# Six norms: feature sums gathered beside the last linear layer's tiles, roots computed with tokens on partitions

## The reference, cut to what matters

```python
def layer_norm(x, g, b):
    mu = jnp.mean(xf, -1, keepdims=True)
    var = jnp.mean(jnp.square(xf - mu), -1, keepdims=True)
    return (xf - mu) * lax.rsqrt(var + NORM_EPS) * g + b
def rms_norm(x, g):
    return xf * lax.rsqrt(jnp.mean(xf * xf, -1, keepdims=True) + EPS) * g
# first_block, i = 0 (attention), 1 (s5):
x = layer_norm(alpha * x + gate * ((y * silu(z)) @ w_out[i]), ln_g[i], ln_b[i])
# hybrid_layer, layer = 0, 1:
hl = rms_norm(xl, norm_mix) * (1.0 + sc1_l) + sh1_l
...
xl = xl + g1_l * (jnp.concatenate([att_l, ml_l, pool_l], -1) @ w_out)
h2l = rms_norm(xl, norm_ffn) * (1.0 + sc2_l) + sh2_l
xl = xl + g2_l * ((silu(h2l @ w_g) * (h2l @ w_u)) @ w_d)
# at the end
return rms_norm(xl, final_norm)
```

## Time and profile before

| | |
|---|---|
| median of three runs | 2534.68 us |
| the three runs | 2533.98, 2534.68, 2544.10 us |
| the profiled execution | 2543.55 us, of it 2541.7 us span |
| granted TensorE clock, mean | 0.921 of full |

### The profile page before, as it was taken

How to read it: one execution, slowest core, us unless ns; L and a number is a source line. 1 busy time by engine, 2 the same in 40 slices (tenths; PEclk the granted TensorE clock), 3 DMA queues, 4 the chain that set the end, 5 groups by cost and what they waited for, 6 DMA issues and landing times.

```text
span 2541.7 us, 33862 instructions
## 1 busy us (share of the span) xinstructions
PE 2211.3 (87%) x13593; PEld 1672.4 (66%) x13593; DVE 1337.6 (53%) x2599; ACT 906.5 (36%) x1779; POOL 443.0 (17%) x417
## 2 busy tenths in 40 slices
PE   6979798879989995699898976889999997878998
PEld 5757576647546694599463433678888764547997
DVE  4648686565479847364425356443333244455554
ACT  3234454552222363353222444232222212444443
POOL 0047878509821000000000000000000000000000
PEclk8979898989999997899899987989999998978999
DMA  8154444685687646865621212322323422224653
GB/s 285 65 183 129 143 144 111 189 258 166 204 267 229 203 150 246 285 183 164 198 68 50 86 48 84 126 89 84 99 84 94 121 83 83 83 83 135 197 161 105
DMA packets 434035, 366.34 MB, mean 144 GB/s; under 512 B 66238, under 2 KB 412622, under 8 KB 431702
## 3 DMA queue, kind: packets, MB, share of 16 engines
q1 hardware_dynamic: 392212, 320.87, 40.9%
q0 software_dynamic: 7424, 26.38, 2.8%
q10 hardware_dynamic: 34242, 16.92, 2.3%
HBM read 317.58 MB, written 54.92 MB: 147 GB/s over the span
## 4 chain that ended last, share of the span: by engine, by line
PE 69%; DVE 14%; DMA 6%; ACT 6%; POOL 3%; issue 2%; ACTq 1%; SPq 0%; DVEq 0%; POOLq 0%
PE ps L119 66%; DVE A L88 3%; PE ps L122 3%; ACT A L115 3%; POOL A L88 3%; DVE R L88 2%; DVE A L102 2%; DMA wbuf<-ctab 2%; DVE A L92 1%; DVE A L105 1%; DVE A L93 1%; DMA wbuf<-in_ada_w 1%; DMA A<-btab 1%; DVE A L96 1%; ACT A L116 1%
## 5 line engine op out<-in xcount | busy, mean ns | idle before, releaser
L119 PE MATMUL ps<-R,R 128*128 128x256 f32 (+1 forms) x3968 | 849.0, 336 | 33.5 <-ACT R L115 23.4
L119 PEld LDWEIGHTS ps<-R,R 128*128 128x128 f32 x3968 | 634.7, 194 | 108.1 <-ACT R L115 28.6
L119 PE MATMUL ps<-HR,R 128*128 128x512 f32 (+1 forms) x1984 | 557.8, 365 | 35.4 <-DVE R L88 24.8
L88 DVE TENSOR_TENSOR R<-wbuf,R 128x1024 fp32r<-128x1024 f32 (+2 forms) x304 | 349.5, 1158 | 368.0 <-ACT R L115 367.8
L119 PEld LDWEIGHTS ps<-HR,R 128*128 128x128 f32 x1984 | 358.9, 194 | 94.7 <-issue 28.5
L115 ACT ACTIVATE A<-ps 128x512 f32<-128x512 f32 (+4 forms) x400 | 210.3, 556 | 583.9 <-PE ps L119 419.3
L115 ACT ACTIVATE R<-wbuf 128x1024 fp32r<-128x1024 f32 (+2 forms) x304 | 270.1, 894 | 293.6 <-PE ps L119 266.9
L88 DVE TENSOR_TENSOR A<-A 128x128 f32<-128x128 f32 (+4 forms) x868 | 320.6, 400 | 88.1 <-ACT A L115 58.6
L119 PE MATMUL ps<-H,wbuf 128*128 128x512 f32 (+2 forms) x928 | 336.6, 520 | 13.8 <-DVE H L93 13.8
L119 PE MATMUL ps<-A 128*128 128x64 f32 (+10 forms) x1736 | 290.0, 369 | 33.3 <-DVE A L88 7.6
L88 POOL TENSOR_TENSOR A<-A 128x512 f32<-128x512 f32 (+3 forms) x186 | 215.4, 1170 | 528.2 <-DVE A L96 268.4
(11 more groups left out here) (103 smaller groups left out, 1644.0 us busy)
## 6 DMA issues: line engine op xcount, KB each, us to landing
wbuf<-in_w_ada SPq DMA_DIRECT2D x48, 1024.0 KB, 5.2
wbuf<-in_ada_w SPq DMA_DIRECT2D x24, 1024.0 KB, 8.5
wbuf<-in_w_out SPq DMA_DIRECT2D x24, 1024.0 KB, 5.7
wbuf<-in_w_ffn_gate SPq DMA_DIRECT2D x22, 1024.0 KB, 5.3
wbuf<-in_w_ffn_up SPq DMA_DIRECT2D x22, 1024.0 KB, 5.7
wbuf<-in_w_ffn_down SPq DMA_DIRECT2D x32, 704.0 KB, 4.7
wbuf<-in_attn_w_in SPq DMA_DIRECT2D x20, 1024.0 KB, 7.0
ctab<-A ACTq DMA_DIRECT2D x64, 256.0 KB, 2.8
```

The costliest lines, as they stand in the source:

```text
L88: return self.op(lambda e: e.tensor_tensor(out, a, b, op))
L119: return self.op(lambda e: e.matmul(out, lhsT, rhs, start=start, stop=stop, skip_group_check=True))
```

## The change

Six of the seven norms change; `b0m1`, whose context half comes from a load, stays.

- **Gather.** The tiles of `out1`, `out2`, `b0out`, `b1out`, `fd0` and `fd1` get `after` work. In the RMS norms ACT squares tile m into `H` and DVE adds tiles 0 to 5 into one accumulator `ACC`, five additions; tiles 6 and 7 stay apart. In the LayerNorms DVE adds `X` tiles 0 to 5 themselves.
- **LayerNorm.** The mean takes three products (`ACC`, `X` 6, `X` 7) in place of eight. The rest is as before.
- **RMS sums.** The squares are now the stationary side and two columns of ones the moving side, so the sums stand with tokens on partitions: 12 products of 2 columns for 512 tokens, 6 for 256, the last third waiting for tile 7's square.
- **Roots.** Scaling, root and reciprocal work on 128x4 or 128x2 in `SM`. DVE multiplies the identity by them into a diagonal `DG` (128 x width), and one product with `ones` spreads it to all partitions, into a PSUM bank that the loop over the eight tiles reads in place of SBUF.
- **Order.** The root moves ahead of `backlog`; one step of `backlog` stands between the sums and the spreading product, and one fewer behind it.

The diff, cut to its core:

```diff
+        SQG, ACC, DG, RT = H[:, 0:2, :], H[:, 2, :], H[:, 3, :], SM[:, 48:52]
+        class Gather:
+            def __init__(self, name, tiles, m, c0, squares):
+                self.name, self.tiles, self.m, self.c0, self.squares = name, tiles, m, c0, squares
+            def act(self, act):
+                m, c0 = self.m, self.c0
+                if self.squares:
+                    act.wait_ge(dve_evac, (self.tiles, m))
+                    if m > 2:
+                        act.wait_ge(dve_step, (self.name, "acc", min(m - 2, 5)))
+                    act.act((ACC if m == 0 else SQG[:, m % 2, :])[:, c0:512], X[:, m, c0:512], ACT.Square
+                            ).then_inc(act_step, (self.name, "sq", m))
+            def dve(self, dve):
+                m, c0 = self.m, self.c0
+                if 1 <= m <= 5:
+                    first, x = ACC, X[:, m, :]
+                    if self.squares:
+                        dve.wait_ge(act_step, (self.name, "sq", m))
+                        x = SQG[:, m % 2, :]
+                    elif m == 1:
+                        first = X[:, 0, :]
+                    dve.wait_ge(dve_evac, (self.tiles, m))
+                    if m > 1:
+                        dve.wait_ge(dve_step, (self.name, "acc", m - 1))
+                    dve.tt(ACC[:, c0:512], first[:, c0:512], x[:, c0:512], ADD).then_inc(dve_step, (self.name, "acc", m))
+            def pe(self, pe):
+                pass
...
+        def gathered_pe(pe, name, c0):
+            p = PS.take(pe, (name, "ss"), (dve_evac, (name, "rs")))
+            for i, (src, ready) in enumerate([(ACC, (dve_step, (name, "acc", 5))), (SQG[:, 0, :], (act_step, (name, "sq", 6))),
+                                              (SQG[:, 1, :], (act_step, (name, "sq", 7)))]):
+                pe.wait_ge(*ready)
+                for j in range(c0 // 128, 4):
+                    x = pe.mm(p[:, 2 * j:2 * j + 2], src[:, 128 * j:128 * j + 128], ones[:, 0:2], i == 0 and j == c0 // 128, i == 2)
+            x.then_inc(mm_done, (name, "ss"))
+        def gathered_dve(dve, name, c0, eps):
+            n = 4 - c0 // 128
+            rt = RT[:, 0:n]
+            dve.wait_ge(mm_done, (name, "ss"))
+            src = PS[name, "ss"][:, 2 * (4 - n):8].rearrange("p (j x) -> p j x", x=2)[:, :, 0]
+            dve.ts(rt, src, 1.0 / D, eps, MUL, ADD).then_inc(dve_evac, (name, "rs"))
+            dve.wait_ge(act_step, (name, "rs"))
+            dve.recip(rt, rt).then_inc(dve_step)
+            dve.wait_own()
+            dve.tt(DG[:, 0:128 * n].rearrange("p (j c) -> p j c", j=n), ident.unsqueeze(1).to_broadcast([128, n, 128]),
+                   rt.unsqueeze(2).to_broadcast([128, n, 128]), MUL).then_inc(dve_step, (name, "dg"))
+        def spread_pe(pe, name, c0, last):
+            p = PS.take(pe, (name, "rb"), last)
+            pe.wait_ge(dve_step, (name, "dg"))
+            pe.mm(p[:, c0:512], ones, DG[:, 0:512 - c0], True, True).then_inc(mm_done, (name, "rb"))
         class LayerNorm:
...
+                self.name, self.c0, self.g, self.bcol, self.SQ, self.RS, self.tiles = name, c0, g, bcol, SQ, RS, tiles
             def pe(self, pe):
                 p = PS.take(pe, (self.name, "mu"), (dve_step, (self.name, "d", 7)))
-                for k in range(8):
-                    pe.wait_ge(*self.ready(k))
-                    x = pe.mm(p[:, self.c0:512], ones, X[:, k, self.c0:512], k == 0, k == 7)
+                pe.wait_ge(dve_step, (self.name, "acc", 5))
+                pe.mm(p[:, self.c0:512], ones, ACC[:, self.c0:512], True, False)
+                for k in (6, 7):
+                    pe.wait_ge(dve_evac, (self.tiles, k))
+                    x = pe.mm(p[:, self.c0:512], ones, X[:, k, self.c0:512], False, k == 7)
                 x.then_inc(mm_done, (self.name, "mu"))
                 yield
...
-        def out_tile(name, w, K, m, hi, lo, n, c0, M, gate, ready, tx):
+        def out_tile(name, w, K, m, hi, lo, n, c0, M, gate, ready, tx, norm, squares=True):
             return Tile((name, m), w, K, 128 * m, n, lambda k: hi[:, k, :], lambda k: lo[:, k, :], ready, dve_evac,
-                        dve=lambda dve, p: dve_residual(dve, name, m, p, c0, M, gate, tx))
+                        dve=lambda dve, p: dve_residual(dve, name, m, p, c0, M, gate, tx),
+                        after=Gather(norm, name, m, c0, squares))
...
-                sumsq_pe(pe, "fin", 256, self.SQ)
+                gathered_pe(pe, "fin", 256)
+                spread_pe(pe, "fin", 256, (dve_step, ("fin", 7)))
...
-                act.wait_mark("end")
-                sumsq_act(act, "fin", 256, self.SQ, lambda k: (dve_evac, ("fd1", k)))
-                rsqrt_act(act, self.RS[:, 256:512], ("fin", "rs"))
+                rsqrt_act(act, RT[:, 0:2], ("fin", "rs"))
...
             def dve(self, dve):
                 dve.wait_mark("end")
-                dve.wait_ge(mm_done, ("fin", "ss", 7))
-                rsqrt_dve(dve, self.RS[:, 256:512], PS["fin", "ss"][:, 256:512], D, 1e-6, ("fin", "rs"))
-                dve.wait_ge(dve_step, ("fin", "rs"))
+                gathered_dve(dve, "fin", 256, 1e-6)
+                dve.wait_ge(mm_done, ("fin", "rb"))
                 for k in range(8):
-                    dve.stt(X[:, k, 256:512], X[:, k, 256:512], vec(2, 16 + k), self.RS[:, 256:512], MUL, MUL
+                    dve.stt(X[:, k, 256:512], X[:, k, 256:512], vec(2, 16 + k), PS["fin", "rb"][:, 256:512], MUL, MUL
                             ).then_inc(dve_step, ("fin", k))
...
             def pe(self, pe):
-                sumsq_pe(pe, self.name, self.cc, SQ)
+                if self.ready:
+                    sumsq_pe(pe, self.name, self.cc, SQ)
+                else:
+                    gathered_pe(pe, self.name, self.cc)
+            def pe2(self, pe):
+                if not self.ready:
+                    spread_pe(pe, self.name, self.cc, (dve_step, (self.name, 7)))
...
             def act(self, act):
+                if not self.ready:
+                    rsqrt_act(act, RT[:, 0:4 - self.cc // 128], (self.name, "rs"))
+                    return
...
             def act2(self, act):
-                rsqrt_act(act, RS[:, self.cc:512], (self.name, "rs"))
+                if self.ready:
+                    rsqrt_act(act, RS[:, self.cc:512], (self.name, "rs"))
...
             def dve(self, dve):
-                pass
+                if not self.ready:
+                    gathered_dve(dve, self.name, self.cc, 1e-6)
             def dve2(self, dve):
                 cc, name = self.cc, self.name
-                dve.wait_ge(mm_done, (name, "ss", 7))
-                rsqrt_dve(dve, RS[:, cc:512], PS[name, "ss"][:, cc:512], D, 1e-6, (name, "rs"))
+                rs = RS
+                if self.ready:
+                    dve.wait_ge(mm_done, (name, "ss", 7))
+                    rsqrt_dve(dve, RS[:, cc:512], PS[name, "ss"][:, cc:512], D, 1e-6, (name, "rs"))
+                else:
+                    rs = PS[name, "rb"]
                 dve.wait_ge(act_evac, self.mod)
                 for s in range(2):
                     dve.tt(S1[:, :, s], MOD[:, self.cs:self.cs + 8, s], self.nv, MUL).then_inc(dve_step)
                 dve.wait_own()
+                if not self.ready:
+                    dve.wait_ge(mm_done, (name, "rb"))
                 for k in range(8):
-                    dve.tt(self.Hd[:, k, cc:512], X[:, k, cc:512], RS[:, cc:512], MUL).then_inc(dve_step)
+                    dve.tt(self.Hd[:, k, cc:512], X[:, k, cc:512], rs[:, cc:512], MUL).then_inc(dve_step)
                     dve.wait_own()
...
-                           lambda k: [(dve_lo, (N, "af", k))], None) for m in range(8)]
+                           lambda k: [(dve_lo, (N, "af", k))], None, "fin" if l else "b1m1") for m in range(8)]
...
             on(rm1)
+            step(backlog, l)
             on(second_half(rm1))
-            step(backlog, 3)
+            step(backlog, 3 - l)
...
             on(rm2)
+            step(backlog)
             on(second_half(rm2))
             if l:
                 rest(backlog)
             else:
-                step(backlog, 4)
+                step(backlog, 3)
```

More of the change, by code:

```diff
@@ L668, in build, with __init__ @@
+        def spread_pe(pe, name, c0, last):
+            p = PS.take(pe, (name, "rb"), last)
+            pe.wait_ge(dve_step, (name, "dg"))
+            pe.mm(p[:, c0:512], ones, DG[:, 0:512 - c0], True, True).then_inc(mm_done, (name, "rb"))
         class LayerNorm:
-            def __init__(self, name, c0, g, bcol, SQ, RS, ready):
-                self.name, self.c0, self.g, self.bcol, self.SQ, self.RS, self.ready = name, c0, g, bcol, SQ, RS, ready
+            def __init__(self, name, c0, g, bcol, SQ, RS, tiles):
+                self.name, self.c0, self.g, self.bcol, self.SQ, self.RS, self.tiles = name, c0, g, bcol, SQ, RS, tiles
@@ L1080, in build @@
         OUT2 = Lin3([out_tile("out2", I["w_out"][1], 16, m, GOH, GOL, 256, 256, MODS[1], 16,
```

(7 more changed lines are left out.)

20 lines of the change are left out of this document (11 added, 9 removed).

## The result

The changed kernel took 2507.47 us in the median of four runs (2505.28 to 2512.79), the kernel before beside it 2536.67; the ratio is 0.9886 with a 95% interval of 0.986 to 0.9912. In a later set of runs it was 0.9906 [0.9882, 0.9931]. As differences of the medians these are 29.2 and 25.5 us. Forecast: 2509, range 2504 to 2523, a gain of 26.0 us.

The account below looks back on a forecast made before the run. TensorE, busy 87% of the span, bounds the kernel; what can be won is its waits at the norms. Six places sum to 27.3 us, less 1.3 for the clock: 26.0 off 2534.68 gives 2509 us, range 2504 to 2523.

Parts of the forecast that it names:

- the places: Gains at six norms: `ln1` 4.3, `ln2` 2.1, `b0m2` 5.85, `b1m1` 7.6, `b1m2` 2.6, last norm 4.9; sum 27.3 us.
- the term for the clock: 1.3 us taken off the gain because TensorE's clock may fall before spreading products and `Ada`'s steps; bounds 0 and 9.
- the prediction's own signs: Right: loops 6 to 7 us after TensorE's last tile at `b0m2`, `b1m1`, `b1m2`; wrong: clock rows of 0.5 at spreading products.
- LayerNorms: At `ln1` and `ln2` eight products of the mean become three, gaining 4.3 and 2.1 us; lower end 0 for both.
- gathering: VectorE's 15 additions of 0.69 and 15 of 0.42 us in the tiles are hidden, priced 0; exposed, 16.7 us.
- `b1m2`: 256-token norm: loop 6.7 us after TensorE leaves the last tile, 9.29 before; gain 2.6 us, bound by `Ada`.
- The addition that stands ahead of the next rounding: On VectorE in the tiles: fits at width 256, makes the rounding 0.5 us late at 512, its buffer wanted several us later.
- Narrow products: TensorE's sums in the RMS norms: 12 or 6 products of two columns, 0.28 us each.
- The rival that they would cost as much as wide ones: Narrow sums on TensorE cost 0.86 us (0.43 at 256) each; gain 10, time 2524 us; chance 0.08.
- The rival named the mechanism and the places: TensorE falls to 1.2 GHz soon after its last tile, slowing `Ada`'s step and spreading product: 8.9 us, time 2516; chance 0.12.
- `Ada`'s values: At `b0m2` the last value of `MOD` comes at 6.2 us, after the hidden diagonal; at `b1m2` `Ada` is the bound.
- The loop's reads of PSUM: 32 loop operations in four norms cost 0.1 us by the rows; the skill's estimate was 65 ns each, 2.1 us.

## Why the prediction was right

**The time** lay 1.5 us from the forecast and inside the range, and the mechanism was the forecast one. But the closeness is in part luck: the places give 22.7 us where 26.0 were forecast, the term for the clock was too small, and other stretches made up for it. (The forecast counts from 2534.68, the kernel before beside the changed one took 2536.67.) By the prediction's own signs two places came out wrong: `b0m2` and `b1m1` start their loops at 8.84 and 8.53, not at 6 to 7, and the clock's rows read 0.5 at their spreading products.

**LayerNorms, gathering, `b1m2`:** right to 0.12 us a place. That the gain would travel along with the loads was right and a little low: behind `ln2` TensorE returned 3.57 us earlier, not 2.1, since a fall of the clock that lay on the sums of squares before (6.25 us, with 0.50 granted from 1216 to 1218; now 4.92, all at 1.00) lies elsewhere now. The other kernels with this part show 3.3 to 3.6 there. The addition that stands ahead of the next rounding was read as harmless from the earlier trace rows, and it was.

**Narrow products:** 0.28 us each forecast; twelve took 3.15, 0.26 each. The rival that they would cost as much as wide ones is out.

**The clock:** the term that was mis-sized. 1.3 us were taken for it in the sum, from two falls 7 us after the last wide product against one at 2.5; the runs show 2.7 at `b0m2` and 1.4 at `b1m1`, 4.1 together, and at the last norm up to 0.5, which came and went with the execution. The rival named the mechanism and the places, `Ada`'s step and the spreading product, and at `b0m2` its price too: 1.6 and 0.86 against 1.5 and 0.96 measured (1.94 + 1.87 − 1.07 − 1.24, and 2.06 − 1.10). At `b1m2` it expected 3.5, and there the clock stayed up. The row at 2532.1, the one fall that followed within 2.5 us, was the one to weigh most. The other two say less than was read from them: the trace before has TensorE at wide products again from 678.32 and from 2043.30, ahead of the falls at 678.6 and 2044.0.

**`Ada`'s values** were said to come last at all three norms of the blocks. At `b0m2` the two small operations on them ran at 1617.12, before ACT had written that step's values at 1618.68, so the loop doesn't need these; only at `b1m2` does it. That is why the spreading product could go ahead of `Ada` at two places and not at the third, which the prediction did not see.

**`b1m1`'s table load** was missing from the sum. It cost nothing in the change itself, behind `Ada`'s slow step, and 0.95 us once the clock was up. With both put right `b0m2` and `b1m1` start at 6.20 and 6.19, 0.45 before the forecast 6.65.

**The loop's reads of PSUM** cost nothing, as the groups of the changed kernel show (mean ns behind the busy time):

```profile
L88 DVE TENSOR_TENSOR A<-X,ps 128x512 f32<-128x512 f32 x8 | 5.4, 680 | 4.2 <-PE ps L119 4.2
L88 DVE TENSOR_TENSOR H<-H 128x512 f32<-128x512 f32 x10 | 6.8, 682 | 0.0
```

680 ns from PSUM against 685 from SBUF in the earlier trace rows. By the Trainium skill, VectorE: DVE Perf Modes, "The TRN2 errata", the estimate was 65 ns more for each and 2.1 us in all; the trace doesn't show it at this width.

**What made up for it** in the first trace: 0.3 us behind `ln1`, 2.1 between the LayerNorms, 0.2 behind `ln2` (the extra 1.4, less the 1.2 of the stretch that follows), 0.4 between `b0m2` and `b1m1`, 1.4 in the attention of block 1 and 1.6 ahead of the last norm; with the places' 22.7 that is the 28.5 from `out1` to the end, but for 0.2. The 2.1 didn't come again: between the LayerNorms the first trace has 501.6 us, the second 504.9, the ten others with gathered LayerNorms 504.8 to 505.2, and the two without 503.7 and 503.6, so as a rule this stretch costs 1.1 to 1.5 us of `ln1`'s gain. All these are of the size of the error and of the spread between executions. "Right" here means the mechanism, three of the six places within 0.15 us (`ln1`, `ln2`, `b1m2`), and a sum that other stretches brought close.

## What to carry to other kernels

Sums over tiles can be gathered on an engine that waits anyway; read the wait that stands ahead of each rounding, and whether a doubled operation still fits. Where wide matrix products are replaced by very narrow ones, look at the granted clock behind them before counting the saving, and try the same products with a broader right-hand side. Where the trace shows ACT's table load behind the wait of a root on the critical path, give ACT a root without a wait, so that its table is there.
